# Gathering the paged keys of a sparse-attention decoder step in half tiles, with a 32x32 block transpose in front of 64-column logits

## The chip, the cores and the metric

One core of a Trainium2 chip runs the whole kernel in one launch. The metric is the device time in microseconds (us). The kernel before took 1592.48, 1596.6 and 1599.31 us in three runs; the median is 1596.6 us.

## The reference, cut to what matters

The kernel computes one layer of a decoder trunk for a prompt group (512 tokens) and a sample group (8 requests of 8 tokens each). All of it is in fp32. The change is in one part only, the attention of the sample group over its paged cache.

```python
ik_past = cache_idx_k[page_table].reshape(DB, past, IDX_DIM)
idx, valid = dsa_select(iq, iw, ik_all, q_pos, topk)          # 256 of 2056 keys for every query
k_sel = jnp.where(is_past, cache_k[phys, slot], gather(k, nidx))
v_sel = jnp.where(is_past, cache_v[phys, slot], gather(v, nidx))
logits = jnp.einsum('bthd,btkhd->bthk', q, k_sel) * ATT_SCALE  # 8 heads x 128
logits = logits + rel_bias[rel_bucket(q_pos - idx)]
p = softmax(where(valid, logits, -inf));  out = einsum('bthk,btkhd->bthd', p, v_sel)
```

Each request has 16 pages of 128 keys, found through `page_table`. A page of keys or of values is 128 rows (one per key) of 8 heads x 128 floats: 512 KB. The kernel doesn't gather the chosen keys. It reads all pages, computes all logits and adds a mask that leaves the chosen keys alone, which gives the same softmax. So 128 pages of keys and 128 of values pass through the core.

## The kernel before, in words

The kernel is written by hand, engine by engine: each engine has one block of instructions in program order, and semaphores tie the blocks together. PSUM is split into four single banks and two pairs of banks, handed out in an order that tables at the top of the program fix (`single`, `pair`). `claim` waits until a bank is free, `filled` until it has been written, `drained` until it has been read.

The sample attention stands in the middle of the program, in two groups G of four requests. For each group three stages follow one another:

- **Keys.** 64 pages, in the order page position kp (0 to 15), then request. SyncE (SP) reads the page number from the table into a register and issues one direct DMA for the page into a ring of eight 4 KB-a-partition tiles (`load_page`, L701 to L713). TensorE turns the page around with eight 128x128 transposes, one for each head (L1197), into two banks. ScalarE copies the first bank to the SBUF tile `KTb` (L1510), VectorE the second (L1793). One page later TensorE multiplies: for each head a stationary tile of 32 columns (`QZ`, where only the 8 columns of this request aren't zero) against 128 key columns (L1210), each head of four on its own 32 output partitions, summed over the four requests. An fp32 matmul shows as two records in the trace. After each fourth page VectorE adds bias and mask and writes the logits of 128 key positions to `LS` (L1787).
- **Softmax.** VectorE takes the maximum, ScalarE the exponential, TensorE transposes the probabilities (L1229), and both copy them to `PTs`.
- **Values.** 64 pages in the same ring, request by request; TensorE multiplies a page straight from the ring, 8 heads with 32-column stationary tiles (L1245).

The other work of this region are the "side tiles": products of the input projection that nothing here needs (gates ga and gb, gMLP input su). A side tile is 48 matmuls of 288 columns (L987 to L989) on a pair of banks, and its result goes to a scratch in DRAM. Each second one asks for the next 1 MB chunk of weights, which ScalarE and VectorE split into a high and a low part. The table `SIDE_V` says behind which page of the value stages a side tile stands: nine in each value stage, one in each softmax, three at the start, none in the key stages.

At the start of the region SP issues four key pages, then writes the mask to DRAM (L719), waits, reads it back spread over the partitions (L722), and goes on with the key pages behind that. GpSimd (POOL) only lays out the queries (L897 to L906) and the bias of the new keys there.

## Time and profile before

| | us |
|---|---|
| Three runs | 1592.48, 1596.6, 1599.31 |
| Span of the profiled execution | 1593.2 |
| Key stages, from their first transpose | 464.6 to 580.7 and 705.8 to 812.4 |
| Softmax stages | to 595.8 and to 828.4 |
| Value stages, to the last output transpose | 595.8 to 705.8 and 828.4 to 930 |

No time of its own is given for the profiled execution beside its span; the three runs lie from 0.7 us under that span to 6.1 us over it. The whole page says that TensorE is busy in 92% of the span, but that is a mean over stages with different limits; the region of the change is the third of the span between 445 and 930 us, and it is read stage by stage.

### The profile page before, as it was taken

The page shows a single profiled execution, that of the slowest core. Times are in us where ns is not written, and L with a number is a line of the kernel's source. Part 1 is how long each engine was busy: PE and PEld are TensorE (multiplying, and loading weights), DVE is VectorE, ACT ScalarE, POOL GpSimd, SP SyncE. Part 2 cuts the span into 40 slices and gives each one's busy share as a digit, 9 for nine tenths or more (in the row PEclk, how much of TensorE's full clock was granted, in tenths as well). Part 3 has the DMA queues.
Part 4 walks back from the last instruction along what each step waited for, and adds up shares of the span by engine and source line. Part 5 has one row for each costly group of instructions (what it writes and reads, how often), then busy time and mean ns, then how long its engine had stood idle before and what let it go on. Part 6 is the DMA issues. An engine that isn't in the chain of part 4 may idle for free.

```text
span 1593.2 us, 32571 instructions
## 1 busy us (share of the span) xinstructions
PE 1471.7 (92%) x13518; PEld 1334.5 (84%) x13518; DVE 762.0 (48%) x1030; ACT 511.5 (32%) x818; POOL 234.5 (15%) x371
## 2 busy tenths in 40 slices
PE   7999998979979989899998998899799999999995
PEld 4867798957867778797777998799699999999995
DVE  5288699496514540025540135543555555552123
ACT  4243223324323341023341122122344455442121
POOL 3423234154210000000000000321000110000000
PEclk8899999989999999999999999899799999999998
DMA  5415223122159979999869976133322233223221
GB/s 173 149 27 159 65 80 113 57 96 73 49 188 369 332 249 342 383 358 329 310 223 402 363 258 240 34 125 104 113 80 80 80 90 95 83 98 102 79 83 60
DMA packets 179278, 266.58 MB, mean 167 GB/s; under 512 B 20522, under 2 KB 136539, under 8 KB 178043
## 3 DMA queue, kind: packets, MB, share of 16 engines
q1 hardware_dynamic: 167947, 243.95, 44.5%
q0 software_dynamic: 5104, 11.11, 2.1%
q10 hardware_dynamic: 6080, 9.44, 1.6%
q8 instruction: 107, 1.75, 0.4%
q14 instruction: 40, 0.33, 0.1%
HBM read 240.28 MB, written 24.18 MB: 166 GB/s over the span
## 4 chain that ended last, share of the span: by engine, by line
PE 77%; DVE 8%; DMA 5%; ACT 3%; SPq 2%; issue 2%; POOL 2%; ACTq 0%; DVEq 0%
PE PS L987 14%; PE PS L989 13%; PE PS L988 13%; PE PS L1197 8%; PE PS L1210 4%; PE PS L1245 3%; PE PS L1319 3%; PE PS L1318 3%; PE PS L1317 3%; DMA R<-in_cache_v 3%; PE PS L1028 2%; PE PS L1029 2%; PE PS L1030 2%; PE PS L1173 1%; PE PS L1120 1%
## 5 line engine op out<-in xcount | busy, mean ns | idle before, releaser
L987 PE MATMUL PS<-xn_hi,WH 128*128 128x288 f32 (+1 forms) x1424 | 430.7, 302 | 16.0 <-DVE xn_lo L1614 13.2
L988 PE MATMUL PS<-xn_lo,WH 128*128 128x288 f32 (+1 forms) x1424 | 424.7, 298 | 0.0
L989 PE MATMUL PS<-xn_hi,WL 128*128 128x288 f32 (+1 forms) x1424 | 424.6, 298 | 0.0
L987 PEld LDWEIGHTS PS<-xn_hi,WH 128*128 128x128 f32 (+1 forms) x1424 | 271.1, 190 | 33.1 <-issue 22.2
L988 PEld LDWEIGHTS PS<-xn_lo,WH 128*128 128x128 f32 (+1 forms) x1424 | 271.9, 191 | 0.0
L989 PEld LDWEIGHTS PS<-xn_hi,WL 128*128 128x128 f32 (+1 forms) x1424 | 271.6, 191 | 0.0
L582 DVE TENSOR_TENSOR WL<-W,WH 128x2048 fp32r<-128x2048 f32 (+2 forms) x69 | 145.7, 2112 | 241.6 <-ACT WH L1358 241.6
L1358 ACT ACTIVATE WH<-W 128x2048 fp32r<-128x2048 f32 (+2 forms) x81 | 145.1, 1791 | 90.2 <-PE PS L1319 74.9
L1197 PE MATMUL PS<-CST,R 128*128 128x128 f32 x1024 | 142.7, 283 | 9.8 <-DMA R<-in_cache_k 9.5
L1793 DVE COPY RB<-PS 128x512 f32<-128x512 f32 x128 | 88.3, 691 | 115.7 <-PE PS L1197 115.7
L1197 PEld LDWEIGHTS PS<-CST,R 128*128 128x128 f32 x1024 | 112.1, 143 | 35.9 <-issue 25.7
L1510 ACT ACTIVATE RB<-PS 128x512 f32<-128x512 f32 x128 | 76.4, 597 | 142.7 <-PE PS L1197 142.7
L1319 PE MATMUL PS<-G_hilo,WL 128*128 128x288 f32 x352 | 103.8, 295 | 0.0
L1317 PE MATMUL PS<-G_hilo,WH 128*128 128x288 f32 x352 | 103.6, 294 | 0.0
L1318 PE MATMUL PS<-G_hilo,WH 128*128 128x288 f32 x352 | 103.6, 294 | 0.0
L1028 PE MATMUL PS<-WH,xn_hi 128*128 128x256 f32 (+1 forms) x320 | 95.4, 298 | 3.8 <-POOL WL L582 3.8
L1391 ACT ACTIVATE STG<-PS 128x576 f32<-128x576 f32 (+2 forms) x44 | 23.3, 529 | 235.0 <-PE PS L989 191.2
L1921 DVE SCALAR_TENSOR_TENSOR CV<-CV,VT 128x592 f32<-128x592 f32 x44 | 36.7, 834 | 124.4 <-ACT CV L1584 124.3
L1029 PE MATMUL PS<-WL,xn_hi 128*128 128x256 f32 (+1 forms) x320 | 91.8, 287 | 0.0
L1030 PE MATMUL PS<-WH,xn_lo 128*128 128x256 f32 (+1 forms) x320 | 91.6, 286 | 0.0
L1245 PE MATMUL PS<-R,R 128*32 128x128 f32 x2176 | 72.7, 284 | 18.1 <-DMA R<-in_cache_v 15.5
L1210 PE MATMUL PS<-RB,R 128*32 128x128 f32 x2048 | 84.4, 283 | 3.5 <-DVE RB L1793 3.5
(257 smaller groups left out, 2423.2 us busy)
## 6 DMA issues: line engine op xcount, KB each, us to landing
R<-in_cache_k SPq DMA_DIRECT2D x128, 512.0 KB, 5.3
R<-in_cache_v SPq DMA_DIRECT2D x128, 512.0 KB, 7.0
W<-in_w_in SPq DMA_DIRECT2D x30, 1024.0 KB, 5.4
W<-in_w_up SPq DMA_DIRECT2D x44, 512.0 KB, 4.6
W<-in_w_down SPq DMA_DIRECT2D x16, 704.0 KB, 4.4
x_scratch<-xT SPq DMA_DIRECT2D x2, 2304.0 KB, 9.0
W<-in_w_branch_a SPq DMA_DIRECT2D x4, 1024.0 KB, 7.9
W<-in_w_branch_b SPq DMA_DIRECT2D x4, 1024.0 KB, 6.1
```

The source lines that it names most:

```text
L582: e.tensor_tensor(WL[n % NW][:, 0:c], W[n % NW][:, 0:c], WH[n % NH][:, 0:c].bitcast(F32), ALU.subtract).then_inc(low_count[name][0], 1)
L987: pe.matmul(out, hi[:, k, cols], x.hi_block(n)[:, tokens], start=first, stop=False)
L988: pe.matmul(out, hi[:, k, cols], x.lo_block(n)[:, tokens], start=False, stop=False)
L989: return pe.matmul(out, lo[:, k, cols], x.hi_block(n)[:, tokens], start=False, stop=last)
L1028: pe.matmul(out, xn1.hi_block(k)[:, t], hi[:, k, :], start=(k == 0), stop=False)
L1029: pe.matmul(out, xn1.hi_block(k)[:, t], lo[:, k, :], start=False, stop=False)
L1197: last = pe.transpose(bank('kp', G, n, u)[:, P * i:P * i + P], ring[seq % 8][:, HD * h:HD * h + HD], ident)
L1210: last = pe.matmul(pbank('kl', G, kp)[32 * j:32 * j + 32, u, 0:P], QZ[:, h, 4 * G + bb, :], KTb[(n - 1) % 2][:, h, :], start=(bb == 0), st ...
L1317: pe.matmul(out, hi[:, k, :], gated(n, 0)[:, t], start=(n == 0), stop=False)
L1318: pe.matmul(out, hi[:, k, :], gated(n, 1)[:, t], start=False, stop=False)
L1319: last = pe.matmul(out, lo[:, k, :], gated(n, 0)[:, t], start=False, stop=(n == FB - 1))
L1358: act.activation(WH[n % NH][:, 0:c], W[n % NW][:, 0:c], ACT.Copy).then_inc(S_("high_ready"), 1)
```

## The change

1. **Key loads.** The keys come by an indirect DMA that POOL issues, from a list of row numbers that it works out once (`KROW`: 64 x page number + 2 x lane). One load fetches half a tile for all four requests of a group: partition 32b + i gets two neighbouring keys of request b, 8 KB in one piece. The ring has four such 1 MB tiles on the same memory as the eight pages. A group takes 32 of these loads in place of 64 pages. SP keeps the value pages.
2. **Turning keys around.** VectorE does one 32x32 block transpose of 128x2048 for each half tile, SBUF to SBUF, into a ring of three (`KTB`). TensorE's transposes and both copies out of PSUM are gone.
3. **Logits.** For each half 32 matmuls (64 records) with 64 key columns: four 32-dimension pieces of each head, summed, against a stationary tile (`QB`) that is block-diagonal over the four requests. ScalarE lays out `QB` in 32 small copies. The mask is read through a rearranged view (`by_rest`), since the keys of a tile are in another order.
4. **Side tiles.** Eight and nine of them stand in the key stages (`SIDE_K`), two in each softmax, two at the start, none in the value stages.
5. **Mask.** ScalarE writes it to DRAM and reads it back.
6. **Banks.** Logits and outputs move from the pairs to the single banks, and side tiles alternate over both pairs.

```diff
-    SIDE_V = [two, two, two, three, two, two, three, {4: 1, 10: 1}]
+    SIDE_K = [[1, 3, 5, 7, 9, 11, 13, 14], [0, 2, 4, 6, 8, 10, 12, 13, 14]]
-    put_side(('start',), 3)
+    put_side(('start',), 2)
...
+        KH = [R1[:, 2048 * i:2048 * i + 2048] for i in range(4)]
+        KTB = [blocks(a, 2) for a in (RB[:, 0:2048], R3[:, 0:2048], R3[:, 2048:4096])]
...
+        def key_freed(e, G, n):
+            if n >= 4:
+                e.wait_ge(S_("k_transposed"), 32 * G + n - 3)
+            elif G:
+                e.wait_ge(S_("v_pages_used"), 64 * G - 6 + 2 * n)
...
+        def page_freed(e, G, n):
+            if n < 8:
+                e.wait_ge(S_("k_transposed"), 32 * G + 29 + n // 2)
             else:
-                e.wait_ge(S_("v_pages_used"), 64 * G + n + 1)
+                e.wait_ge(S_("v_pages_used"), 64 * G + n - 7)
...
+        def load_keys(e, G, n):
+            key_freed(e, G, n)
+            kp, a = n // 2, n % 2
+            e.indirect_dma_start(out=KH[n % 4], out_offset=None,
+                                 in_=cache_k[0].rearrange("n (k r) h d -> (n k) (r h d)", r=2),
+                                 in_offset=bass.IndirectOffsetOnAxis(ap=KROW[:, 16 * G + kp:16 * G + kp + 1], axis=0),
+                                 element_offset=2 * D * a).then_inc(key_in[n % 4], 16)
...
+                for kp in range(NPAGES):
+                    claim(pe, 'kl', G, kp)
+                    for a in range(2):
+                        pe.wait_ge(S_("k_transposed"), 32 * G + 2 * kp + a + 1)
+                        keys = KTB[(2 * kp + a) % 3]
                         for u in range(2):
                             for j in range(4):
+                                for c in range(4):
+                                    o = P * u + 64 * a
+                                    last = pe.matmul(bank('kl', G, kp)[32 * c:32 * c + 32, o:o + 64],
+                                                     QB[:, G, 4 * u + c, j, :],
+                                                     keys[:, :, 512 * u + P * c + 32 * j:512 * u + P * c + 32 * j + 32],
+                                                     start=(j == 0), stop=(j == 3))
+                    sides('K', G, kp)
...
+            act.wait_ge(S_("queries_cleared"), 1)
+                        last = act.activation(QB[32 * bb:32 * bb + 32, G, :, j, 8 * bb:8 * bb + 8],
+                                              qT[32 * j:32 * j + 32, :, t:t + 8], ACT.Copy)
+            act.dma_start(mask_scr, S).then_inc(S_("mask_out"), 16)
             sides('start')
...
+                def transposed(kp):
+                    for a in range(2):
+                        n = 2 * kp + a
+                        dve.wait_ge(key_in[n % 4], 16 * (8 * G + n // 4 + 1))
+                        if n >= 3:
+                            if n % 2 == 0:
+                                filled(dve, 'kl', G, (n - 3) // 2)
+                            else:
+                                dve.wait_ge(S_("k_half_used"), 16 * G + (n - 3) // 2 + 1)
+                        dve.transpose(KTB[n % 3], blocks(KH[n % 4], 2))\
+                            .then_inc(S_("k_transposed"), 1)
+                for kp in range(NPAGES):
+                    transposed(kp)
+                    if kp >= 2:
+                        logits(kp - 2)
```

On TensorE, in the key stage before, two pages look like this (`CST` is the identity, `RB` the turned keys, `R_63` the ring, `R_66` the queries; one row of a matmul is two records of the trace):

```order
L1197 MATMUL PS<-CST,R_63 128x128 [waits single_drained3,page_in5]
L1197 MATMUL PS<-CST,R_63 128x128 x3
L1197 MATMUL PS<-CST,R_63 128x128 [waits single_drained0]
L1197 MATMUL PS<-CST,R_63 128x128 x3
L1210 MATMUL PS<-RB,R_66 32x128 [waits single_drained1,pair_drained1]
L1210 MATMUL PS<-RB,R_66 32x128 x3
L1210 MATMUL PS<-RB,R_66 32x128 [waits single_drained2]
L1210 MATMUL PS<-RB,R_66 32x128 x3
```

The same engine now, for the first four half tiles (eight pages' worth) and the first rows of the side tile behind them (`RB` and `R_66` hold the ring of turned keys):

```order
L1219 MATMUL PS<-RB,R_66 32x64 [waits k_transposed,single_drained1,sample_queries]
L1219 MATMUL PS<-RB,R_66 32x64 x31
L1219 MATMUL PS<-R_66 32x64 [waits k_transposed]
L1219 MATMUL PS<-R_66 32x64 x31
L1219 MATMUL PS<-R_66 32x64 [waits k_transposed,single_drained2]
L1219 MATMUL PS<-R_66 32x64 x31
L1219 MATMUL PS<-RB,R_66 32x64 [waits k_transposed]
L1219 MATMUL PS<-RB,R_66 32x64 x31
L1006 MATMUL PS<-xn_hi,WH_61 128x288 [waits pair_drained1,low_ready]
L1007 MATMUL PS<-xn_lo,WH_61 128x288
L1008 MATMUL PS<-xn_hi,WL_60 128x288
```

The transposes have gone, the matmuls have half the columns and twice the number for each key, and each half waits for VectorE alone. On VectorE, before, one round of four pages in the key stage is:

```order
L1793 COPY RB<-PS 128x512 [waits single_filled] x5
L1787 SCALAR_TENSOR_TENSOR R_64<-PS,NBr,SR 128x128 [waits mask_in0,pair_filled0]
L1787 SCALAR_TENSOR_TENSOR R_64<-PS,NBr,SR 128x128
L1793 COPY RB<-PS 128x512 [waits single_filled] x4
L1787 SCALAR_TENSOR_TENSOR R_64<-PS,NBr,SR 128x128 [waits pair_filled1]
```

VectorE now, from the split of a weight chunk on (`key_half_in` is the arrival of a half tile, `single_filled` and `k_half_used` TensorE's end with an earlier half):

```order
L587 TENSOR_TENSOR WL_58<-W_55,WH_62 128x2048 [waits high_ready]
L1836 STREAM_TRANSPOSE R_66<-R_63 128x2048 [waits single_filled,key_half_in0]
L1836 STREAM_TRANSPOSE R_66<-R_63 128x2048 [waits k_half_used,key_half_in1]
L1816 SCALAR_TENSOR_TENSOR R_64<-PS,NBr,SR 128x4x32 [waits mask_in0,single_filled]
L1816 SCALAR_TENSOR_TENSOR R_64<-PS,NBr,SR 128x4x32
L1836 STREAM_TRANSPOSE RB<-R_63 128x2048 [waits single_filled,key_half_in2]
L1836 STREAM_TRANSPOSE R_66<-R_63 128x2048 [waits k_half_used,key_half_in3]
```

Four copies of 512 columns have become two transposes of 2048, and the logits of a tile stand behind the transposes of the tile two further on. POOL, which did nothing in the key stages, now holds the queue of key loads:

```order
L912 MEMSET R_66 128x2048 [waits k_stored0,k_stored1,single_drained0,single_filled]
L640 DMA R_63<-in_cache_k,KROW 128x2048 [waits v_stored,single_filled]
L640 DMA R_63<-in_cache_k,KROW 128x2048
L915 MEMSET R_66 128x8x64
L916 COPY R_66<-R_63 128x8x64 [waits pool_step]
L917 COPY R_63<-R_64 128x512 [waits pool_step]
L918 MEMSET ST 1x1 [waits pool_step]
L640 DMA R_63<-in_cache_k,KROW 128x2048 x2
L926 TENSOR_SCALAR R_64<-NBr 128x128 [waits stored_pool,nbr_in,sample_queries]
L640 DMA R_63<-in_cache_k,KROW 128x2048 [waits k_transposed] x28
```

The first two loads stand directly behind the clearing of the query tile; from the fifth load on each waits for the transpose that frees its place in the ring.

## Rows read from the trace of the kernel before

**Rows 1.** The page: span and busy time of each engine.
```profile
span 1593.2 us, 32571 instructions
PE 1471.7 (92%) x13518; PEld 1334.5 (84%) x13518; DVE 762.0 (48%) x1030; ACT 511.5 (32%) x818; POOL 234.5 (15%) x371
```

**Rows 2.** Windows by stage: length, busy us of each engine (instructions), clock, DMA share, GB/s.
```profile
480.00:580.00 100.00, 98.26 (x1452) 75.05 (x1454) 52.59 (x91) 36.58 (x61) 0.00 (x0) 0.97 0.92 332
595.80:713.00 117.20, 106.50 (x1620) 96.45 (x1624) 16.34 (x17) 16.97 (x26) 0.00 (x0) 0.94 0.94 356
828.00:930.00 102.00, 95.64 (x1529) 88.69 (x1530) 13.98 (x15) 15.41 (x20) 0.00 (x0) 0.97 0.94 357
```

**Rows 3.** Timeline of TensorE in the key stage: start, us, engine, line, operation.
```profile
719.90 1.09 PE L1197 MATMUL PS<-CST,R 128*128 128x128 f32 x8
720.93 0.65 PE L1210 MATMUL PS<-RB,R 128*32 128x128 f32 x16
721.50 1.09 PE L1197 MATMUL PS<-CST,R 128*128 128x128 f32 x8
```

**Rows 4.** Timeline of TensorE in the first value stage.
```profile
595.77 3.70 PE L1245 MATMUL PS<-R,R 128*32 128x128 f32 x128 [1.43 <-DVE R L1817]
599.40 0.40 PE L987 MATMUL PS<-xn_hi,WH 128*128 128x288 f32 x1
605.95 2.61 PE L1245 MATMUL PS<-R,R 128*32 128x128 f32 x80
610.78 0.65 PE L1245 MATMUL PS<-R,R 128*32 128x128 f32 x16 [0.99 <-DMA R<-in_cache_v]
614.66 0.44 PE L988 MATMUL PS<-xn_lo,WH 128*128 128x288 f32 x1
614.90 0.44 PE L989 MATMUL PS<-xn_hi,WL 128*128 128x288 f32 x1
```

**Rows 5.** Windows in the value stages with the highest and a usual DMA rate.
```profile
600.00:620.00 20.00, 17.45 (x219) 15.73 (x218) 0.61 (x2) 0.65 (x1) 0.00 (x0) 0.83 0.98 373
860.00:880.00 20.00, 17.06 (x215) 14.42 (x213) 0.61 (x2) 0.69 (x2) 0.00 (x0) 0.83 0.97 396
```

**Rows 6.** Groups of VectorE by line and shape: busy us, mean ns, idle before.
```profile
L582 DVE TENSOR_TENSOR WL<-W,WH 128x2048 fp32r<-128x2048 f32 x52 | 119.0, 2288 | 140.8 <-ACT WH L1358 140.7
L1793 DVE COPY RB<-PS 128x512 f32<-128x512 f32 x128 | 88.3, 691 | 115.7 <-PE PS L1197 115.7
L1787 DVE SCALAR_TENSOR_TENSOR R<-PS,NBr,SR 128x128 f32<-128x128 f32 x68 | 20.5, 345 | 1.5 <-PE PS L1210 1.5
```

**Rows 7.** Chain of waits: the early maximum on VectorE.
```profile
552.87 3.35 DVE ST L1799
```

**Rows 8.** Groups of POOL by line: busy us, mean ns, idle before.
```profile
L620 POOL DMA_DIRECT2D R<-in_cache_idx_k x64 | 34.7, 542 | 70.0 <-issue 42.3 <-PE PS L1107 20.3 <-PE PS L1113 7.3
L901 POOL MEMSET R<- 128x2048 f32 x1 | 1.8, 1813 | 0.0
```

**Rows 9.** Issues: DMAs, KB each, median us from issue to landing.
```profile
out<-R POOLq DMA_DIRECT2D x1, 2048.0 KB, 10.4
```

**Rows 10.** Timelines of POOL and SP at the start of the region.
```profile
445.08 0.53 POOL L897 MEMSET R<- 128x512 f32 x1 [36.17 <-PE PS L1173]
458.31 3.79 SPq L711 DMA_DIRECT2D R<-in_cache_k  x4
470.21 1.92 SPq L722 DMA_DIRECT2D SR<-mask_scratch  x4
```

**Rows 11.** Timelines of TensorE and ScalarE in the first softmax.
```profile
581.05 0.37 PE L987 MATMUL PS<-xn_hi,WH 128*128 128x288 f32 x1 [0.39 <-DVE R L1787]
586.48 2.10 ACT L1514 ACTIVATE R<-R,ST 128x2176 f32<-128x2176 f32 x1
587.49 1.91 PE L1229 MATMUL PS<-CST,R 128*128 128x128 f32 x16
```

**Rows 12.** Timeline at the end of the second value stage.
```profile
929.71 0.44 PE L1256 MATMUL PS<-CST,R 128*128 128x128 f32 x2 [0.73 <-DVE R L1826]
```

More of the change, by code:

```diff
@@ L223, in hybrid_kernel @@
     for G in range(2):
-        for n in range(64):
-            single.add('kp', G, n, 0)
-            single.add('kp', G, n, 1)
         for kp in range(NPG):
-            pair.add('kl', G, kp, at=kp % 2)
-        for i, tile in enumerate(side_at['softmax', G, 0] + side_at['softmax', G, 1]):
-            pair.add(*tile, at=(i + 1) % 2)
+            single.add('kl', G, kp)
+            for tile in side_at.get(('K', G, kp), ()):
+                pair.add(*tile)
+        for tile in side_at['softmax', G, 0] + side_at['softmax', G, 1]:
+            pair.add(*tile)
         for g in range(2):
@@ L234, in hybrid_kernel @@
         for b in range(4):
-            pair.add('o', G, b, at=0)
+            single.add('o', G, b)
             for kp in range(NPG):
                 for tile in side_at.get(('V', G, b, kp), ()):
-                    pair.add(*tile, at=1)
+                    pair.add(*tile)
             single.add('ot', G, b, 0)
             single.add('ot', G, b, 1)
-    pair.add(*side[-1], at=1)
+    for tile in side_at['end',]:
+        pair.add(*tile)
     for c in range(8):
@@ L1786, in logits @@
                     for g in range(2):
[L1787 to L1797 removed]
+                        out, mask = LS[:, g, P * kp:P * kp + P], MG[:, P * kp:P * kp + P]
```

167 lines of the change are left out of this document (80 added, 87 removed).

## The prediction

> **What bounds the kernel now.** I read four views. First the page's head: TensorE is busy in 92% of 1593.2 us [rows 1]. Next the windows, cut at the stages: in the key stage TensorE is busy 98.3 of 100 us while DMA moves 332 GB/s; in the value stages it is busy 106.5 of 117.2 and 95.6 of 102 us, with DMA at 356 and 357 GB/s [rows 2]. Then the timelines of TensorE. A key page repeats every 1.60 us (719.90 to 721.50): 8 transposes, 1.09 us, then 16 records of logits, 0.65 us, hardly overlapping [rows 3]. Nothing is waited for there, so the key stage is TensorE's: 64 x 1.60 = 102 us, of which the transposes hold about two thirds. In the value stage, once the eight pages of the ring are used up, single pages of 16 records stand with a wait of about 1 us for the next page [rows 4]: between side tiles DMA sets the pace. Last the windows of 20 us, which say what DMA can do there: 373 GB/s is usual, 396 the best [rows 5].
>
> So neither stage uses both resources fully. 128 pages of 0.524 MB a group are 67.1 MB, 181 us at 370 GB/s, and while the first group's key and value stages take 116.1 and 109.9 us, 226 us (the table of stages above; the values begin at 595.77 [rows 4], the last ends at 929.71 [rows 12]). The change takes two thirds of TensorE's key work away, and fills the room with the side tiles of the value stage.
>
> **The unit costs.** *Transposes and copies removed:* 64 pages a group x 1.09 us on TensorE, 64 x 0.691 us on VectorE [rows 3, 6], and the same number on ScalarE, which had time to spare.
>
> *New logits:* 32 halves of 64 records. 128-column records with 32 stationary columns start every (3.70 - 0.27)/127 = 27 ns in a long run, and every (0.65 - 0.27)/15 = 25 ns in a burst of 16 (0.27 us is the tail of the last record) [rows 3, 4]. With 64 columns the bounds are 13.5 ns (half) and 27 ns (no gain). Four column groups work side by side in both forms; what goes on to cost is issue and weight load, which don't shrink, so I take 25 ns, the value of the shortest burst. The Trainium skill (TensorE: Matmul & The Clock Gate, "Wait — 56ns, not 53.3ns?") says that start to start never drops below about 25 ns however few columns there are. By that rule halving the columns gains nothing, and the trace, which shows no start closer than 25 ns, doesn't contradict it; without the rule TensorE's part of a half would be 0.9 us and not 1.6. A half is 64 x 0.025 = 1.6 us, plus 0.15 us for the turn to the next semaphore, the rest of the 1.60 us page that neither row explains: 1.75 us, 56 us a group. Bounds: 33 and 60 us.
>
> *Side tile:* 599.40 to 605.95 is 6.5 us at the full clock (2.4 GHz), one record each 0.136 us. From 614.66 to 614.90 a record stands 0.24 us from the next, in a stretch whose granted clock is 0.83 on the mean: there it ran at 1.2 GHz, and a tile takes 11.5 us [rows 4, 5].
>
> *Block transpose:* 128x2048 fp32, not in this trace. The nearest row is the split of a chunk, the same shape from SBUF to SBUF: 2.29 us [rows 6], so 2.29. A lower bound is half, 1.15 us, if it took two elements a cycle; the upper one is 4.4 us, if fp32 took two cycles.
>
> *Gather:* 1 MB from POOL, also unseen. POOL's plain DMAs hold it 0.54 us [rows 8], and one of 2 MB landed in 10.4 us [rows 9]. Lower bound: the best rate of rows 5, 1.05/396 = 2.6 us a half. Upper: 5.2 us a half, the pace of that lone POOL transfer, if gathers don't overlap. With four in flight and 8 KB pieces I take 2.8 us.
>
> **The key stage, summed.** For two key positions (four halves, one side tile):
> - TensorE: 4 x 1.75 + 6.5 = 13.5 us.
> - VectorE: 4 x 2.29 + 4 x 0.345 for the logits + half a split, 1.15 = 11.7 us [rows 6], all told 97 us a group with the early maximum. That maximum is 3.35 us once a group [rows 7].
> - DMA: 4.2 MB of keys, 0.5 MB of weights, 0.3 MB of stored result = 5.0 MB, 13.5 us at 370 GB/s.
>
> The three lie so near each other that the buffers matter. Behind a side tile VectorE may be three halves ahead (3 x 2.29 = 6.9 us, about the 6.5 us of the tile); these feed TensorE for 5.2 us, while VectorE makes the next within 1.75 + 2.29 = 4.0. So TensorE doesn't wait, and 8 x 13.5 = 108 us, 110 with the extra maximum and ends. The second group has nine side tiles and begins cold: 116 us. Before: 116.1 and 106.6 us.
>
> **Start.** POOL was free at 445.1; the first key page went out at 458.3 behind SP's weight chunk, and the mask's trip over DRAM, whose last load SP issued at 472.1, then held page 5 and those behind it back [rows 10]. Now POOL clears 1.8 us [rows 8] and issues two halves at about 447. ScalarE's 32 copies, of 64 elements, take 11 us at the 0.345 us of a 128-element VectorE operation [rows 6], so the queries stand at 458, before the first half is turned. Two side tiles rather than three stand ahead of the keys, and VectorE has a split (2.29 us) in front. First logits at 462; the mask is needed only for the third key position, some 12 us on. It is hidden unless ScalarE is over 10 us late.
>
> **Softmax.** The side tile ran from 581.05 to 587.49, while the first exponential was ready about 586.5 [rows 11], so the first tile is nearly free and the second isn't: + 6.5 us, less some 2 us because ScalarE will be past its second exponential. 20 us a group in place of 15.1 and 16.
>
> **Value stage.** Nothing but DMA: 8 pages (4.2 MB) are there at its start, 56 x 0.524 = 29.4 MB remain, at 385 GB/s (between rows 5's two) 76 us, + 4 us until the freed ring delivers again = 80 us. TensorE's 0.43 us a page, even at half its clock 0.86 us, is under the 1.36 us of a page. Before: 109.9 and 101.3 us. SP issues a page every 0.95 us (four in 3.79 [rows 10]), fast enough. The clock will be at 1.2 GHz here for the most part, since it already fell (0.83) with side tiles in between; I add 2 us for a cold start behind the second group.
>
> **The sum, along the time axis:** 462 + 110 = 572; softmax 592; values 672; 3 us until keys queued behind the last values have come, + 116 = 791; softmax 811; values 891; cold 2: 893. The last output transpose is at 929.7 now [rows 12]. Gain 37 us. The span 1593.2 lies inside the three runs and 3.4 us under their median, so 1596.6 - 37 = 1560 us.
>
> **Rivals.**
> *A, the gather is slow.* Mechanism: key loads are one POOL queue, in line, and none of the next 28 goes out before a transpose frees its place. The gain of 37 us is gone when the two key stages grow by 18.5 us each, at (110 + 18.5)/32 = 4.0 us a half. At the upper bound, 5.2 us a half, a key stage is 166 us: + 56 and + 50, so 1560 + 106 = 1666. For it: indirect loads appear nowhere in the trace, and the pace of the lone POOL transfer. Against: four tiles in flight, large pieces. The Trainium skill (SBUF — State Buffer, "Who interferes with whom") holds that a two-port VectorE operation locks GpSimd out while it writes descriptors; it names copy, cast and tensor_scalar, not the transpose. No row here shows a POOL issue beside such an operation. If each issue did wait for a transpose, the period would be 2.29 + 0.54 held + 0.66 between POOL's issues (42.3 us over 64 [rows 8]) = 3.5 us, 112 us a stage: 2 us on the sum at most.
> *B, the transpose takes two cycles an element.* VectorE: 32 x 4.4 + 24 = 165 us a key stage; + 55 and + 49: 1664 us. The gain is gone from (128.5 - 24)/32 = 3.3 us a transpose on. For: nothing in the rows; against: every fp32 VectorE row runs at 1 element a cycle.
> *C, the handshake doesn't overlap.* VectorE isn't ahead when the side tile ends (late loads, late splits): a pair costs 6.5 + 4 x 2.29 = 15.7 us, 125 us a stage; + 15 and + 13: 1588 us.
> *D, no floor at 25 ns, DMA at its best.* TensorE 33 + 52 = 85 us; VectorE (97) and DMA (40.3 MB at 396: 102) then bind: key stages 102 and 106, value stages 77: gain 37 + 18 + 6 = 61: 1536 us.
>
> **Chances.** Forecast 0.61 (own range 1543 to 1580), A 0.10, B 0.06, C 0.12, D 0.11. Of A and B 0.01 at milder sizes counts as no change. C is split: 0.06 faster, 0.04 no change, 0.02 slower; of the forecast 0.03 counts as no change and 0.02 as slower. Faster by over 0.5% (8 us, what a measurement can tell here): 0.73; within 0.5%: 0.08; slower: 0.19. The range 1530 to 1612 leaves out A, B and little else.
>
> **What would show it.** Right: STREAM_TRANSPOSE near 2.3 us; records of 64 columns every 25 ns; POOL's indirect issues under 2.5 us apart when free; value stages near 80 us with 370 to 400 GB/s and TensorE waiting for pages; a key stage of 105 to 120 us with TensorE over 90% busy. Wrong: TensorE waiting for VectorE over 10 us a group with VectorE waiting for key halves (A, by the DMA rate under 300 GB/s), or with VectorE full (B); waits only behind side tiles (C). If the value stages stay over 95 us, the room that I see there isn't there.

## The result, and the profile after

The changed kernel takes 1583.84 us (median of 8 runs, 1577.16 to 1593.04), the kernel before 1592.2 us (8 runs, 1589.3 to 1599.31). The ratio is 0.9941, 95% interval 0.9914 to 0.9968. So it is faster, by 8 us; I had forecast 37, and the time lies 4 us above the upper end of the forecast's own range (1543 to 1580). The kernel before came out at 1592.2 in eight runs, where the forecast had started from 1596.6, the median of three.

The page of the changed kernel, head and groups (columns as in [rows 1] and [rows 6]):

```profile
span 1582.7 us, 33691 instructions
PE 1385.6 (88%) x14542; PEld 1258.0 (79%) x14542; DVE 821.1 (52%) x966; ACT 444.3 (28%) x722; POOL 299.2 (19%) x430
...
L1258 PE MATMUL PS<-R,R 128*32 128x128 f32 x2176 | 104.5, 331 | 57.2 <-DMA R<-in_cache_v 53.9
...
L1836 DVE STREAM_TRANSPOSE R<-R 128x2048 f32<-128x2048 f32 x42 | 96.0, 2295 | 31.3 <-PE PS L1219 20.4
L640 POOL DMA_INDIRECT R<-in_cache_k,KROW x64 | 64.1, 1001 | 250.5 <-PE PS L1258 98.1
```

Against [rows 1] TensorE is busy 86 us less, but the span is only 10.5 us shorter: most of the work that went left standing time behind. The stages, read from TensorE's timeline. For the changed kernel a stage runs from its first record of logits or values to its last; for the one before the key stage begins with the first transpose and ends behind the logits of the new keys, and the value stage ends at the last output transpose, as in the table ahead of the prediction. The difference is 0.4 us at the end of a key stage and about 1 us at the end of a value stage, too little to change a reading:

| us | before | forecast | after |
|---|---|---|---|
| Keys 0 | 464.6 to 580.7: 116.1 | 462 to 572: 110 | 461.9 to 586.2: 124.3 |
| Softmax 0 | 15.1 | 20 | 19.2 |
| Values 0 | 109.9 | 80 | 85.5 |
| up to the next keys | 0.1 | 3 | 3.0 |
| Keys 1 | 106.6 | 116 | 122.3 |
| Softmax 1 | 16 | 20 | 19.2 |
| Values 1 | 101.3 | 82 | 79.9 |
| last output transpose | 929.7 | 893 | 916.2 |

The value stages gained what was forecast, less 5.5 us. The key stages, which were to shrink by 6 and grow by 9 us, grew by 8 and 16. Windows of both, as [rows 2] (PE, PEld, DVE, ACT, POOL busy with counts, clock, DMA share, GB/s):

```profile
470.00:570.00 100.00, 79.06 (x1873) 73.86 (x1873) 71.96 (x53) 9.64 (x9) 24.01 (x25) 0.87 0.95 345
...
605.40:690.90 85.50, 53.73 (x1094) 32.73 (x1094) 1.83 (x6) 0.92 (x6) 2.92 (x3) 0.77 1.03 405
835.50:915.50 80.00, 52.88 (x1094) 32.79 (x1094) 1.83 (x6) 0.92 (x6) 0.00 (x0) 0.79 0.94 369
```

In the key stage TensorE was busy in 98.3 us of 100 before [rows 2] and is in 79.1 now, VectorE in 72.0: neither is full, although DMA is near it (share 0.95). Its timeline says where it stands (start, us, engine, line, operation; in brackets the idle time before and what ended it):

```profile
472.39 1.44 PE L1219 MATMUL PS<-RB,R 128*32 128x64 f32 x42 [3.42 <-issue]
...
488.43 0.86 PE L1219 MATMUL PS<-RB,R 128*32 128x64 f32 x26 [1.34 <-issue]
...
499.71 1.11 PE L1219 MATMUL PS<-RB,R 128*32 128x64 f32 x64
...
506.57 0.64 PE L1219 MATMUL PS<-R 128*32 128x64 f32 x13 [3.06 <-issue]
```

The third row is an undisturbed half: 64 records in 1.11 us, one every (1.11 - 0.22)/63 = 14 ns on the mean (0.22 us is the length of one). In the others TensorE stops in the middle of a half, where it waits for no semaphore: 42 records come 3.42 us behind the 22 of the same half, which had begun at 468.43. The waits of TensorE, then of VectorE, between 464 and 586 us (us in total, times, longest):

```profile
PE PS L1219 <- issue: 18.2, 11, 3.7
PE PS L1219 <- DVE RB L1836: 1.8, 3, 0.9
PE PS L1219 <- DVE R L1836: 1.4, 3, 0.7
```

```profile
DVE RB L1836 <- PE PS L1219: 11.7, 2, 7.0
DVE R L1836 <- DMA R<-in_cache_k,KROW: 9.0, 3, 6.6
DVE R L1836 <- PE PS L1219: 6.9, 4, 2.2
```

VectorE waits for TensorE, which waits for "issue", that is for nothing that this view shows. In the second key stage it is the same, 17.4 us in 15 pauses. During or behind five of the eight pauses over 0.5 us of the first key stage the granted clock falls to 1.2 GHz (at 471.5, 488.6, 505.6, 550.0 and 567.1) for 3 to 7 us, and a side tile that begins there takes up to 9.0 us rather than 6.5:

```profile
507.14 0.61 PE L1006 MATMUL PS<-xn_hi,WH 128*128 128x288 f32 x1
...
508.03 0.44 PE L1006 MATMUL PS<-xn_hi,WH 128*128 128x288 f32 x1
508.75 0.44 PE L1006 MATMUL PS<-xn_hi,WH 128*128 128x288 f32 x1
...
514.40 0.29 PE L1006 MATMUL PS<-xn_hi,WH 128*128 128x288 f32 x1
514.80 0.29 PE L1006 MATMUL PS<-xn_hi,WH 128*128 128x288 f32 x1
```

Rows of this line are three records apart: 0.72 us until about 512, 0.40 later. The eight tiles of the first key stage took 8.7, 6.9, 9.0, 6.6, 8.2, 8.6, 7.7 and 6.6 us, 62 in place of 52 (1.3 us of it is a pause inside the fifth).

Counted in records, the pauses over 1.2 us of the first key stage lie 255, 382, 509, 128, 255 and 254 apart, near 2, 3, 4, 1, 2 and 2 times 128. 128 records are 256 instructions, since each has its weight load. The page has a queue for the supply of instructions, before, after, and in the experiment "pairs" below (packets, MB, share of the engines; a second queue of the same kind moved 0.3 MB in each):

```profile
q8 instruction: 107, 1.75, 0.4%
```

```profile
q8 instruction: 114, 1.87, 0.5%
```

```profile
q8 instruction: 98, 1.61, 0.4%
```

"pairs" has 2048 records, so 4096 instructions, fewer than the changed kernel, and 16 packets fewer: 256 instructions, 16 KB, a packet. A pause at such borders, where 512 instructions go by in about 4 us, looks like an engine that has used up what was fetched.

The trace also holds the times of single packets, and they bear the reading out. The six longest pauses of the first key stage (us):

| TensorE stops | the packet starts | the packet is in | TensorE goes on |
|---|---|---|---|
| 468.96 | 469.69 | 470.97 | 472.39 |
| 487.08 | 485.90 | 487.00 | 488.43 |
| 503.50 | 504.23 | 505.11 | 506.57 |
| 530.84 | 530.39 | 531.35 | 532.66 |
| 547.54 | 548.98 | 549.86 | 551.28 |
| 563.59 | 564.04 | 565.06 | 566.32 |

Each of the 14 pauses over 0.5 us of the two key stages ends 1.26 to 1.48 us behind a packet of queue q8; so do, within 1.1 to 1.7 us, all 103 of them in the key stages of this kernel and of the experiments. The short pauses, of up to 0.4 us (1.5 us in all in the first stage), follow no packet. In no trace here do two packets start less than 3.3 us apart. 256 instructions in 3.3 us are 128 records, 26 ns each: an estimate from these rows of what comes in when packets follow each other as closely as here, against the 14 ns at which the new records are used up.

### The profile page after: what moved, and what is told of

Read it like the earlier page. It is cut to its first block, busy times and chain, and to the rows that moved or that the text cites. A ratio compares the mean times of both kernels' runs of the same rounds, so it can differ in the third digit from the quotient of the medians.

```text
span 1582.7 us, 33691 instructions
## 1 busy us (share of the span) xinstructions
PE 1385.6 (88%) x14542; PEld 1258.0 (79%) x14542; DVE 821.1 (52%) x966; ACT 444.3 (28%) x722; POOL 299.2 (19%) x430
## 3 DMA queue, kind: packets, MB, share of 16 engines
q0 software_dynamic: 14320, 78.22, 13.5%
## 4 chain that ended last, share of the span: by engine, by line
PE 69%; DMA 10%; DVE 9%; issue 5%; ACT 3%; SPq 2%; POOL 2%; ACTq 0%; DVEq 0%
PE PS L1006 15%; PE PS L1007 14%; PE PS L1008 14%; DMA R<-in_cache_v 7%; PE PS L1219 4%; PE PS L1333 3%; PE PS L1331 3%; PE PS L1332 3%; PE PS L1048 2%; PE PS L1047 2%; PE PS L1049 2%; PE PS L1192 1%; PE PS L1258 1%; DMA R<-in_cache_k,KROW 1%; PE PS L1139 1%
## 5 line engine op out<-in xcount | busy, mean ns | idle before, releaser
L1006 PEld LDWEIGHTS PS<-xn_hi,WH 128*128 128x128 f32 (+1 forms) x1424 | 275.3, 193 | 30.6 <-issue 18.8
L1258 PE MATMUL PS<-R,R 128*32 128x128 f32 x2176 | 104.5, 331 | 57.2 <-DMA R<-in_cache_v 53.9
L1258 PEld LDWEIGHTS PS<-R,R 128*32 128x32 f32 x2176 | 64.3, 128 | 96.3 <-DMA R<-in_cache_v 88.9
L1836 DVE STREAM_TRANSPOSE R<-R 128x2048 f32<-128x2048 f32 x42 | 96.0, 2295 | 31.3 <-PE PS L1219 20.4
L640 POOL DMA_INDIRECT R<-in_cache_k,KROW x64 | 64.1, 1001 | 250.5 <-PE PS L1258 98.1
L1874 DVE TENSOR_SCALAR R<-PS,ST 128x128 f32<-128x128 f32 x16 | 4.9, 347 | 162.1 <-PE PS L1258 162.1
L1219 PE MATMUL PS<-R 128*32 128x64 f32 x2688 | 54.3, 230 | 29.0 <-issue 25.6
```

Source lines behind the costliest of these rows:

```text
L1006: pe.matmul(out, hi[:, k, cols], x.hi_block(n)[:, tokens], start=first, stop=False)
L1258: last = pe.matmul(bank('o', G, b)[32 * j:32 * j + 32, HD * u:HD * u + HD], PTs[:, u, kp, 32 * j:32 * j + 32], page[:, HD * h:HD * h + HD] ...
```

## The experiments

The first four runs were made to test one theory (I in the expectations): the gathers load the DMA engines, which fetch the instructions too, and so TensorE stands; against it stood P, that TensorE itself doesn't hold 14 ns a record, and Q, that the bytes queued count. After them came J: the number of records itself is too much for the supply, whatever else the DMA does; and C, rival C of the prediction: TensorE and VectorE wait for each other, whole side tiles long. Each kernel is the changed one with the edit shown. Stage times of their profiled executions, us ("pauses" are the waits of TensorE for issue in the two key stages):

| kernel | keys 0 / 1 | values 0 / 1 | pauses 0 / 1 | time, median |
|---|---|---|---|---|
| changed | 124.3 / 122.3 | 85.5 / 79.9 | 19.5 / 17.9 | 1583.84 |
| small_gather | 113.6 / 112.4 | 83.6 / 80.3 | 15.0 / 10.7 | 1560.48 (one run) |
| gather_4k | 127.7 / 127.1 | 84.1 / 80.0 | 14.1 / 18.7 | 1588.74 |
| two_in_flight | 149.4 / 146.6 | 84.4 / 79.9 | 4.6 / 3.4 | 1632.18 |
| sides_in_values | 92.8 / 85.9 | 109.5 / 105.3 | 8.4 / 18.9 | 1566.49 |
| half_records | 107.7 / 103.4 | 87.4 / 80.5 | 1.5 / 1.8 | 1549.83 (one run) |
| split_tiles | 117.0 / 120.7 | 85.7 / 79.3 | 14.6 / 20.4 | 1572.46 |
| mask_first | 121.3 / 124.2 | 85.1 / 79.1 | 17.5 / 17.3 | 1584.21 |
| mixed | 108.3 / 106.1 | 97.8 / 97.5 | 22.6 / 22.4 | 1581.53 |
| pairs | 111.4 / 113.2 | 86.8 / 79.7 | 0 / 0 | 1568.47 |
| pairs_split | 100.5 / 105.1 | 86.1 / 80.0 | 0 / 0 | 1547.5 |
| pairs_values | 96.7 / 91.1 | 106.2 / 107.8 | 0 / 0 | 1577.56 |
| pairs_mixed_split | 97.8 / 93.9 | 96.4 / 88.9 | 0 / 0 | 1557.64 |

**small_gather.** A load fetches 2 KB in place of 8 KB for each partition, so three quarters of every turned half are old data (the row numbers are scaled to match, not shown).

```
-            e.indirect_dma_start(out=KH[n % 4], out_offset=None,
-                                 in_=cache_k[0].rearrange("n (k r) h d -> (n k) (r h d)", r=2),
+            e.indirect_dma_start(out=KH[n % 4][:, 0:512], out_offset=None,
+                                 in_=cache_k[0].rearrange("n k (u h) d -> (n k u) (h d)", u=2),
```

> The changed kernel, but each gather brings 2 KB a partition in place of 8 KB, so a quarter of the key bytes; three quarters of every turned half tile are old data. Everything else is issued as before. In the changed kernel the key stages take 124.7 and 122.7 us, with 18.2 and 17.4 us in which TensorE stands in the middle of a half and waits for nothing that the profile shows. Theory I (its instructions come late, since the DMA that brings them shares the DMA engines with the gathers): these pieces fall from about 2 to 4 us each to under 1 us, some 5 us a stage or less, and the key stages end near 100 us, held by VectorE (32 x 2.30 + 24 = 98 us). Rival P (TensorE itself can't hold 14 ns a record, or semaphores cost it): the pieces stay, 15 us or more a stage, and the key stages stay over 112 us.

The same window as above:

```profile
470.00:570.00 100.00, 84.08 (x2067) 80.03 (x2067) 82.21 (x62) 10.31 (x10) 23.71 (x25) 0.91 0.39 121
```

With the DMA share at 0.39 the pauses are still there, 15.0 and 10.7 us, the longest 3.8 and 4.0 us, as long as in the changed kernel. The instruction packets took 1.10 and 1.05 us on the mean in its two key stages, against 1.02 and 1.00 in the changed kernel: lighter traffic doesn't speed them up. So busy DMA engines are not what makes TensorE stop (I falls as the main cause). The sum of pauses fell by 4.5 and 7.2 us all the same, in one execution. All told the traffic of the keys costs 10.7 and 9.9 us in the two stages.

**gather_4k.** Two gathers of 4 KB a partition for each half.

```
+            for r in range(2):
+                e.indirect_dma_start(out=KH[n % 4][:, D * r:D * r + D], ...
+                                     element_offset=2 * D * a + D * r)
```

> Each half tile is gathered by two indirect DMAs of 4 KB a partition in place of one of 8 KB; same bytes, twice the issues on POOL (about 1 us each). Theory I with turns taken piece by piece on a DMA engine: a smaller piece in front of the instructions halves the wait for them, the unexplained waits on TensorE fall from 18 and 17 us to about 10 a stage, the kernel is 10 to 15 us faster than the changed one. Theory Q (what counts is how many bytes are queued, not the size of a piece): waits and time as in the changed kernel within 4 us. If POOL's issue is the bound, key stages grow by over 10 us.

The ratio to the kernel before is 0.9976 (0.996 to 0.9993): the medians lie 4.9 us above the changed kernel, with intervals that overlap. POOL was held 1.03 us by each of the 128 loads, twice as long in all. The key stages were 3.4 and 4.8 us longer, the pauses 14.1 and 18.7 us in place of 19.5 and 17.9: theory I had them at 10 and the kernel 10 to 15 us faster. The size of the pieces doesn't decide.

**two_in_flight.** A load waits for the transpose two places back rather than four.

```
-            if n >= 4:
-                e.wait_ge(S_("k_transposed"), 32 * G + n - 3)
+            if n >= 2:
+                e.wait_ge(S_("k_transposed"), 32 * G + n - 1)
```

> A gather waits until at most one earlier half is not yet turned: two gathers in flight in place of four. Theory Q (depth of the queue delays the instructions): unexplained waits on TensorE halve, to about 9 us a stage, but VectorE waits more for keys; key stages 120 to 135 us. Theory I by turns: the unexplained waits stay at 15 us or more a stage, and VectorE's waits come on top: key stages over 130 us, kernel 10 to 25 us slower than the changed one.

1632.18 us, ratio 1.0256 (1.0229 to 1.0284), 48 us slower than the changed kernel; the worst that I had expected was 25. VectorE's waits between 464 and 586 us:

```profile
DVE R L1834 <- DMA R<-in_cache_k,KROW: 36.0, 16, 8.7
DVE RB L1834 <- DMA R<-in_cache_k,KROW: 10.8, 7, 2.5
```

This is what a key stage looks like that the loads bound (rival A): VectorE waits 47 us for keys in that window, against 9 in the changed kernel, 268 GB/s between 470 and 570 us, a stage of 149 us. And the pauses have nearly gone, one of 4.6 and one of 3.4 us: TensorE has more time for the same records.

**sides_in_values.** The key part alone: the side tiles stand where they stood before.

```
+    SIDE_V = [two, two, two, three, two, two, three, {4: 1, 10: 1}]
+    SIDE_K = [[], []]
-    put_side(('start',), 2)
+    put_side(('start',), 3)
-        put_side(('softmax', G, 0), 2)
+        put_side(('softmax', G, 0), 1)
```

> The key part of the change alone: the side tiles stand where they were before the change (three at the start, one in each softmax, nine in each value stage, none in the key stages). Theory as predicted (the key stage is three resources close together, and the side tiles are what it gains by): key stages VectorE-bound at about 100 us, value stages back at 110 and 101, softmax 15 and 16: last output transpose at 464 + 100 + 15 + 110 + 100 + 16 + 101 = 906 us, 10 us faster than the changed kernel. Rival: late instructions cost the same without side tiles, 18 us a stage on top of TensorE's 32 us, which VectorE's 98 hide: the same number, but with TensorE idle. If the key stages stay over 110 us, it is the gathers' rate that holds them.

1566.49 us, ratio 0.9833 (0.9808 to 0.9857). I had thought it about 10 us faster than the changed kernel; it is 17 faster. Moving the side tiles, which was half of the change, cost 17 us. The pauses are there (18.9 us in the second stage) but they delay little: the key stage is VectorE's now. Windows of 480 to 560 and 700 to 780 us:

```profile
480.00:560.00 80.00, 47.03 (x1680) 41.59 (x1683) 72.05 (x54) 0.00 (x0) 21.55 (x23) 0.63 0.98 371
700.00:780.00 80.00, 49.06 (x1867) 43.63 (x1859) 77.85 (x60) 0.00 (x0) 23.84 (x26) 0.68 0.98 389
```

VectorE is busy in 72.1 and 77.9 of 80 us, and 32 x 2.30 + 32 x 0.38 (0.77 us for two logits) + 3.4 = 89 us is its work; the stage takes 85.9 from TensorE's first record to its last, with the last logits behind that.

**half_records.** Only the first two of the four 32-dimension pieces of each head.

```
-                            for j in range(4):
+                            for j in range(2):
-                                                      start=(j == 0), stop=(j == 3))
+                                                      start=(j == 0), stop=(j == 1))
```

> Only two of the four 32-dimension pieces of each head are summed, so half of the dimensions are left out of the past logits; a half tile is 32 records on TensorE in place of 64. Loads, transposes, masks and side tiles as in the changed kernel. In the changed kernel and in the one with a quarter of the key bytes TensorE stands still inside a half 7 to 11 times a key stage, 15 to 19 us in sum, about every 128 or 256 records. Theory J (the supply of instructions: four halves in a row use 512 instructions in 4 us, more than come in): with half the records these pieces all but vanish, under 4 us a stage, and the key stages are 105 to 112 us, of which 16 us less is TensorE's own work (1.0 us a half becomes 0.5). Theory C (TensorE and VectorE wait for one another across a side tile, whatever the instructions): the key stages stay within 5 us of 124 and 122, with the waits between the two engines larger.

With half the records the pauses fall to 1.5 and 1.8 us, none over 0.4 us, at an unchanged traffic (350 GB/s in the window of 470 to 570 us), and a half still runs at 14 ns a record (32 in 0.65 us). J holds: what counts is how many records come in a row, and P, that TensorE can't hold the pace, falls. But TensorE did half the logits' work too, so 1549.83 us doesn't say what the pauses cost.

**split_tiles.** Each side tile of the key stages as two halves, in two key positions.

```
+            def key_sides(G, kp):
+                for kind, c in side_at.get(('K', G, kp), ()):
+                    if kp == 0:
+                        column_part(kind, c, 0)
+                    column_part(kind, c, 1)
+                for kind, c in side_at.get(('K', G, kp + 1), ()):
+                    column_part(kind, c, 0)
-                    sides('K', G, kp)
+                    key_sides(G, kp)
```

> Each side tile of a key stage is done in two halves of 24 matmuls, one behind the key position in front of its old place and one at its old place, so TensorE alternates 2 us of logits with 3.3 us of side work. Theories C and J both: VectorE, with a ring of three, is never left idle for a whole tile, and the instruction bursts are half as long; waits of VectorE for TensorE fall from 18 us to under 6 us a stage and the pieces without reason under 8 us: key stages 110 us, kernel 20 to 28 us faster than the changed one. Rival T (the clock: TensorE falls to 1.2 GHz whenever it is not dense): tiles still take 8 us, key stages 118 us or more.

1572.46 us, ratio 0.9868 (0.9839 to 0.9897), 11 us faster than the changed kernel, where I had expected 20 to 28, with as many pauses (14.6 and 20.4 us). While a whole side tile runs VectorE fills its ring of three and stands; with half tiles its longest wait for TensorE in the first key stage is 3.6 us in place of 7.0. But that doesn't show C in the changed kernel: TensorE, which sets the pace there, waits for VectorE 3.2 and 1.8 us a stage, and 3.7 and 0 with half tiles. Of the 11 us the traces show 9 in the key stages and 2.5 ahead of the first logits; what gives the 9 stays open.

**mask_first.** ScalarE writes the mask out ahead of its 32 copies and of the side tiles.

```
+            act.wait_ge(S_("sample_mask"), 1)
+            act.dma_start(mask_scr, S).then_inc(S_("mask_out"), 16)
...
-            act.wait_ge(S_("sample_mask"), 1)
-            act.dma_start(mask_scr, S).then_inc(S_("mask_out"), 16)
```

> ScalarE writes the mask to DRAM before its 32 query copies and reads it back before the side tiles of the start, so that the 1.1 MB read no longer meets the fifth and sixth gather. In the changed kernel VectorE waits from 470.5 to 477.2 for the fifth half and then 1.5 us more. Theory M (that wait is the mask's read in the same DMA engines): the wait falls to under 2 us, the first key stage to about 118 us, and the kernel is 5 to 7 us faster. Rival: the gather issued at 462 is late for another reason (POOL's issue, the weight chunk): no difference beyond 2 us.

1584.21 us, ratio 0.9943 (0.9921 to 0.9965): no difference to the changed kernel, where I had expected 5 to 7 us. The one wait of 6.6 us for the fifth half, which fell together with the return of the mask, broke up into short ones (6.2 us in all, the longest 2.0), and the time was lost elsewhere.

**mixed.** Three and four side tiles in the key stages, five in each value stage.

```
+    SIDE_V = [{4: 1, 10: 1}, {7: 1}, {7: 1}, {7: 1}, {4: 1, 10: 1}, {7: 1}, {7: 1}, {7: 1}]
+    SIDE_K = [[3, 7, 11], [3, 7, 11, 14]]
```

> Side tiles spread: three and four in the key stages, five in each value stage, two in each softmax, two at the start. With all in the values the stages were 94 and 86 us (keys), 110 and 105 (values); with all in the keys 124 and 122, 86 and 80. If a tile costs the same wherever it stands (3.8 us in the keys, 2.8 in the values), keys are 105 and 102, values 100 and 94: last output transpose at 462 + 105 + 19 + 100 + 3 + 102 + 19 + 94 = 904, no better than all in the values. Theory (each stage has room that costs nothing until one resource is full): keys 98 and 95, values 90 and 86: 874 us, and the kernel 1540 to 1550 us, 40 us under the one before.

I took TensorE to have free room in the value stages, since it waits there for DMA. That missed: 1581.53 us, ratio 0.9925 (0.9897 to 0.9954). Five tiles, 32 us of TensorE, lengthen the value stages by 12.3 and 17.6 us. TensorE's free time there is waits of about 0.6 us for single pages, 49 of them in the first value stage; pieces of 6.5 us don't fit into them. That is how I read it, no run has smaller pieces there alone.

**pairs.** The test of J without leaving work out: TensorE multiplies both halves of a key position at once, 128 columns a record, half the records for the same products. Not shown: the loads of the two halves are swapped at every third position, so that both stand in order in the ring, and VectorE waits for TensorE's end with a whole pair, no longer with a half.

```
-                    for a in range(2):
-                        pe.wait_ge(S_("k_transposed"), 32 * G + 2 * kp + a + 1)
+                    pe.wait_ge(S_("k_transposed"), 32 * G + 2 * kp + 2)
+                    lo, hi = sorted((KAT[2 * kp % 3], KAT[(2 * kp + 1) % 3]))
...
+                                 last = pe.matmul(bank('kl', G, kp)[32 * c:32 * c + 32, P * u:P * u + P],
+                                                  QB[:, G, 4 * u + c, j, :],
+                                                  bass.AP(w.tensor, w.offset, [w.ap[0], [hi - lo, 2], [1024, 2], [1, 32]]),
```

> The same work as the changed kernel with half the records: TensorE waits for both halves of a key position and multiplies 128 columns at once (4 x 32, out of two places of the ring of three), 64 records for a position in place of 128. VectorE can then run only one and a half halves further ahead. 128-column records take 27 ns, so TensorE's own work stays 1.8 us a position (2.0 before). Theory J (supply of instructions): pieces without reason fall from 18 us to under 4 us a stage as with half the arithmetic left out, key stages 105 to 112 us, kernel 20 to 30 us faster than the changed one. Rival: the longer wait of TensorE for VectorE eats it: pieces vanish, key stages 118 us or more.

1568.47 us, ratio 0.986 (0.9831 to 0.989): 15 us faster than the changed kernel, where I had expected 20 to 30. TensorE's waits from 464 us to the end of the first key stage:

```profile
PE PS L1220 <- DVE KALL L1831: 28.0, 10, 7.2
```

No pause is left in either stage. What came in its place is a wait for VectorE, since both transposes must be done first: of the 28.0 us 7.2 lie ahead of the first logits, 20.8 in the stage, and 17.1 in the second. The timeline, from one side tile to the next:

```profile
510.27 1.95 PE L1220 MATMUL PS<-KALL,R 128*32 128x128 f32 x64
514.82 3.32 PE L1220 MATMUL PS<-KALL,R 128*32 128x128 f32 x64 [2.60 <-DVE KALL L1831]
```

64 records of 128 columns take 1.95 us at 2.4 GHz, one every 27 ns on the mean: the columns per ns are those of the 14 ns records. At 1.2 GHz, behind a wait, it is 3.32.

**pairs_split.** The edits of pairs, split_tiles and mask_first together.

> As pairs, with the side tiles of the key stages done in halves of 24 matmuls around each position, and the mask written and read early. Theory J plus C: with few instructions VectorE is the bound (98 us) and nothing leaves it idle for long: key stages 100 to 106 us, kernel 1540 to 1550 us. If the clock is what is left, tiles take over 7.5 us on the mean and the stages stay over 108.

1547.5 us (1540.8 to 1551.27), ratio 0.9714 (0.9683 to 0.9744): the fastest of all, 36 us below the changed kernel and 45 below the one before. The two key stages:

```profile
480.00:560.00 80.00, 68.86 (x1096) 64.01 (x1100) 75.22 (x55) 9.77 (x10) 21.55 (x23) 0.98 1.01 400
700.00:780.00 80.00, 69.65 (x1080) 65.10 (x1076) 73.19 (x55) 14.48 (x13) 18.73 (x20) 0.98 1.01 395
```

VectorE is busy 94 and 91% and DMA moves 400 and 395 GB/s: both are near their end, and the clock is up (0.98). VectorE's work of 97 us a stage in the prediction stands against a measured 100.5 and 105.1. TensorE's waits for VectorE inside the stages fell from 20.8 and 17.1 us in pairs to 12.2 and 10.3, and the stages from 111.4 and 113.2. Here half tiles do what rival C says, once no pause hides it (the mask's part was nothing in mask_first).

**pairs_values.** The edits of pairs and sides_in_values together.

> Pairs, with the side tiles in the value stages as before the change. With 64-column records and the same places the stages were 94 and 86 (keys), 110 and 105 (values). TensorE has 60 us of idle time in such a key stage, so fewer records should do nothing there: keys 92 and 86, time within 5 us of that kernel's 1566.5 us. If keys fall under 84 us, the instruction supply counted there too.

I expected what sides_in_values gives, within 5 us. That missed: it is 11 us slower, 1577.56 us, ratio 0.9909 (0.9877 to 0.9942). Without side tiles the stage is VectorE's, and a ring of three is too short for pairs: VectorE can't turn a second half of the next pair before TensorE has done with both of the last.

```profile
DVE KALL L1836 <- PE PS L1225: 7.4, 10, 1.0
```

That wait isn't there in sides_in_values. It and a later start of each pair make the key stages 3.9 and 5.2 us longer. The rest of the 11 us I have not traced.

**pairs_mixed_split.** pairs_split with five side tiles in each key stage and seven in the value stages.

```
+    SIDE_V = [{7: 1}, {7: 1}, {7: 1}, {7: 1}, {7: 1}, {7: 1}, {7: 1}, {}]
+    SIDE_K = [[2, 5, 8, 11, 14], [2, 5, 8, 11, 13]]
```

> Pairs, split side tiles, early mask, five side tiles in each key stage and seven in the values. Keys: DMA 38 MB at 385 is 99 us, VectorE 95, so 97 and 95 us; values 90 and 88: last output transpose at 460 + 97 + 19 + 90 + 3 + 95 + 19 + 88 = 871 us, kernel 1535 to 1548. If a tile costs 2.5 us or more in the value stages although DMA sets the pace there, as in the kernel with mixed places, it comes to 1550 or more and all in the keys is better.

1557.64 us, ratio 0.9783 (0.9754 to 0.9812), above the 1535 to 1548 that I had expected and 10 us slower than pairs_split: 13.9 us won in the key stages, 19.2 lost in the value stages. Once the key stages run without pauses, they are the better place for the side tiles, as the change had it.

## Why the prediction was wrong

The direction held, the size did not: 37 us forecast, 8 measured. Along the axis of its sum:

- **Start, 462.** Right: 461.94. In seven of the experiments it was 458.1 to 463.4, so the hit to 0.1 us is luck. Two halves issued at 447, and the queries were in time.
- **Key stage, 110 and 116 us.** The term that failed: 124.3 and 122.3, + 14 and + 6, 20.6 of the 23 us by which the last output transpose came later than forecast (916.2 for 893). The step was "TensorE: 4 x 1.75 + 6.5 = 13.5 us" with the conclusion "TensorE doesn't wait". It was wrong twice over. A half takes 1.0 us and not 1.75: records of 64 columns start every 14 ns on the mean, the lower one of my bounds, while I took 25 ns from the shortest burst of the trace. By the right duration alone rival D would have held: 32 + 52 = 84 us for TensorE, the stage bound by VectorE and DMA. But records at that pace go by faster than the instructions come: 19.5 and 17.9 us of pauses. Then the clock, down behind most of the long pauses: the tiles of the first stage took 62 us for 52, and TensorE was busy 42 us with logits for 32. 42 + 62 + 18.2 (pauses outside the tiles) + 3.2 (waits for VectorE) = 125 for the stage of 124.3 us, since logits and tiles overlap a little. In the forecast the same sum was 56 + 52 and nothing for pauses, waits and clock. I had counted TensorE's busy time and its semaphores, and nothing for where its instructions come from. No row of before asks as much: its densest run is 128 records in 3.70 us [rows 4], now 128 take some 2 us.
- **The handshake, rival C (1588 us, 0.12).** Nearest in its number, but by luck: in the changed kernel TensorE waited only 3.2 and 1.8 us a stage for VectorE, which the rival has it wait for behind each side tile. My sentence that VectorE is three halves ahead behind a side tile was true, but that is also the end of the ring: it then waits itself, 18.6 and 18.9 us a stage. With the pauses gone this counts: from pairs to pairs_split, with half tiles, the stages lost 11 and 8 us. Half tiles alone won 11 us on the changed kernel, by a way that the traces don't settle.
- **Softmax, 20.** 19.2 and 19.2.
- **Value stage, 80.** 79.9 in the second group. A page comes every 1.28 us there, 0.524 MB / 1.28 = 410 GB/s, better than the 1.36 us of the sum. In the first it was 85.5: the keys of the next group are issued as its last pages come free, and 2.9 MB of them moved while the last request ran, whose 16 pages took 24.4 us and those of the others 19.4. I had put 3 us for keys that come late and nothing for values that wait for them. The keys' bytes are not all of it: with a quarter of them (small_gather) the last request still took 22.2 us and the stage 83.6; the rest stays open.
- **The cold start of 2 us** was not seen in the region. Behind it the changed kernel takes 666.5 us from its last output transpose to the end and the one before 663.5, at a granted clock that is 0.03 lower in the 100 us that begin 40 us behind it (0.88 against 0.91). That takes the 13.5 us won in the region down to the 10.5 of the span. Why the clock is lower there stays open.
- **Rival A, slow gathers.** No. A load holds POOL 0.94 us (median), and the key stages of pairs_split moved 400 GB/s. With a shallower ring it is real: two in flight cost 48 us.
- **Rival B, two cycles an element.** No: 2.30 us a transpose, as the forecast's 2.29.
- **The value pages on SP** stood behind a weight chunk until 585.5. All eight were there when the values began at 605.4, so it cost nothing; no kernel tests it.

The Trainium skill (TensorE: Matmul & The Clock Gate, "Wait — 56ns, not 53.3ns?") puts a floor of about 25 ns under the distance of two starts. The runs contradict it for this form, 128x64 with 32 stationary columns and four column groups in turn: 14 ns on the mean, in each undisturbed half. By that rule I had lowered the chance of D. My sentence that the trace before shows no start closer than 25 ns was a misreading: 25 and 27 ns are means. In its bursts of 16 [rows 3] the four column groups start 6 or 7 ns apart, with a step of 89 ns or more behind each four, so that one group starts again after 109 ns; with 64 columns it does after 56 ns. A distance of 25 ns from one start to the next was no floor there either.

The Trainium skill (SBUF — State Buffer, "Who interferes with whom") has GpSimd locked out by some VectorE operations. The block transpose is none of them here: 19 of the 64 loads lie wholly inside transposes and hold POOL 0.93 to 1.01 us. One of them in two rows of the changed kernel:

```profile
461.72 4.46 DVE L1836 STREAM_TRANSPOSE R<-R 128x2048 f32<-128x2048 f32 x2
...
464.26 0.95 POOL L640 DMA_INDIRECT R<-in_cache_k,KROW  x1 [1.17 <-DVE R L1836]
```

What is shown and what not: that the number of records makes the pauses is shown by pairs (same products, half the records, no pauses, 15 us) and half_records. That TensorE then stands for want of instructions is read from the borders of 256 and from the times of the packets, 103 pauses of 103; no run changed the fetch itself. Why a packet starts only when it does, in four of the six rows above after TensorE has stopped, stays open. Of the 21 us that the key stages took beyond the forecast, pairs gives back 22 and brings waits of 21 and 17 us for VectorE with it, split tiles give 9; the shares don't add up to a clean account.

## What to carry to other kernels

When an edit makes TensorE's instructions shorter, count how many instructions a microsecond it then asks for, not only their busy time: a wide record does the same work with half the supply. A pause in a run of equal instructions that waits for "issue" and ends behind an instruction packet is its mark. And when work is moved into a stage of two engines with a short ring between them, cut it into pieces no longer than the ring lasts; here that and the wide records turned 8 us into 45.

## What the runs showed of the hardware

- fp32 records of 128x64 with 32 stationary columns, on four column groups in turn, start every 14 ns on the mean at 2.4 GHz and every 27 ns with 128 columns: the time goes by the columns down to there.
- TensorE stood still 0.6 to 3.7 us at many of the borders of 128 records when up to four halves of 14 ns records came in a row, 18 and 20 us a stage with the short pauses; it went on 1.26 to 1.48 us behind the landing of a 16 KB instruction packet. With half the records (128 columns each, or half of the pieces) no such pause came.
- Instruction packets start at least 3.3 us apart in all 14 traces.
- A 32x32 block transpose of 128x2048 fp32 takes 2.30 us. An indirect load of 128 rows holds POOL 0.94 us, with 8 KB a row as with 2 KB.
- With four gathers of 1 MB in flight the key stages of pairs_split moved 400 GB/s in all, with two in flight those of two_in_flight 268.
